# A deep fused kernel (RWKV-7, differential attention, two hybrid layers): tails and output stages in another order, table load behind the Silu, score matmuls by halves

## The reference

```python
def diff_attention_blocks(q, k_all, v_all, lam):      # 8 heads, each with two halves of 64
    s = jnp.einsum("bqhcd,bkhcd->bchqk", q_blk, k_all) * scale   # c: the two halves; 768 keys
    p = jax.nn.softmax(s, axis=-1)
    attn = p[:, 0] - lam * p[:, 1]
    return jnp.einsum("bhqk,bkhe->bqhe", attn, v_all)
def diff_finish(o, g, subln, lam_init, w_out):
    y = rms_norm(o, subln, SUBLN_EPS) * (1.0 - lam_init)
    return (y.reshape(B, T, DA_VW) * jax.nn.silu(g)) @ w_out
```

## Time and profile before

| | |
|---|---|
| runs (us) | 2391.37, 2387.86, 2383.27; median 2387.86 |
| the profiled execution, its time | 2388.85 us |
| its span, first to last instruction | 2387.0 us |
| mean granted TensorE clock | 0.962 of full speed |
| busy: PE, DVE, ACT, POOL | 86%, 55%, 47%, 30% |
| DMA | mean 93 GB/s |

### The profile page before, as it was taken

The page is one execution under the profiler, slowest core; times in us unless marked ns, Lnnn a source line. Parts: engine busy times, 40 slices in busy tenths (PEclk is TensorE's granted clock), DMA queues, the critical chain, the costliest instruction groups (busy, mean ns, idle before and its releaser), DMA issues.

```text
span 2387.0 us, 56898 instructions
## 1 busy us (share of the span) xinstructions
PE 2058.7 (86%) x24624; PEld 1583.7 (66%) x24624; DVE 1304.5 (55%) x2181; ACT 1118.4 (47%) x1861; POOL 708.8 (30%) x417
## 2 busy tenths in 40 slices
PE   6999998688878888878899999979899889899889
PEld 3877776567666677656676666647566666666666
DVE  3288787634334444443456667672566652466752
ACT  5476676433333343332354454553455453455552
POOL 2344544100022030233332222333433332443433
PEclk9999999899999999998999999989999989899999
DMA  7233646633332322223131111103222211222122
GB/s 298 89 121 122 185 131 186 184 99 91 113 102 72 83 67 74 60 96 124 60 105 55 54 45 58 54 23 115 75 67 79 65 61 71 71 80 71 62 71 71
DMA packets 162313, 221.35 MB, mean 93 GB/s; under 512 B 84592, under 2 KB 116336, under 8 KB 161296
## 3 DMA queue, kind: packets, MB, share of 16 engines
q1 hardware_dynamic: 151920, 177.99, 24.4%
q0 software_dynamic: 8992, 36.57, 5.1%
q10 hardware_dynamic: 1152, 3.15, 0.4%
HBM read 164.98 MB, written 42.21 MB: 87 GB/s over the span
## 4 chain that ended last, share of the span: by engine, by line
PE 57%; DVE 19%; ACT 12%; issue 8%; POOL 3%; DMA 1%; ACTq 0%; DVEq 0%; POOLq 0%; SPq 0%
PE ps L272 8%; PE ps L274 7%; PE ps L273 7%; PE ps L1605 3%; PE ps L1595 2%; PE ps L1627 2%; PE ps L421 2%; DVE Y L1768 2%; PE ps L2607 2%; PE ps L2545 1%; PE ps L3186 1%; ACT DE L1725 1%; ACT p L2627 1%; PE ps L3144 1%; DVE pc L3262 1%
## 5 line engine op out<-in xcount | busy, mean ns | idle before, releaser
L257 POOL TENSOR_TENSOR wbl<-wb,wbh 128x1024 fp32r<-128x1024 f32 x122 | 294.6, 2416 | 652.7 <-ACT wbh L251 652.7
L1768 DVE COPY_PREDICATED Y<-rc,ps 128x512 f32<-128x512 int32 x120 | 85.5, 732 | 196.3 <-ACT DE L1725 135.0
L272 PE MATMUL ps<-hT2h,wbh 128*128 128x512 f32 x416 | 180.5, 434 | 10.6 <-POOL wbl L257 10.6
L272 PE MATMUL ps<-hTh,wah 128*128 128x512 f32 (+1 forms) x512 | 179.5, 351 | 10.9 <-POOL wal L257 10.9
L273 PE MATMUL ps<-hTl,wah 128*128 128x512 f32 (+1 forms) x512 | 173.8, 340 | 0.0
L274 PE MATMUL ps<-hTh,wal 128*128 128x512 f32 (+1 forms) x512 | 173.6, 339 | 0.0
L274 PE MATMUL ps<-hT2h,wbl 128*128 128x512 f32 x416 | 164.6, 396 | 0.0
L273 PE MATMUL ps<-hT2l,wbh 128*128 128x512 f32 x416 | 164.0, 394 | 0.0
L1942 POOL TENSOR_TENSOR ro<-ro 128x768 f32<-128x768 f32 x6 | 10.9, 1813 | 496.8 <-DVE ro L365 496.8
L251 ACT ACTIVATE wbh<-wb 128x1024 fp32r<-128x1024 f32 x122 | 128.2, 1052 | 61.9 <-PE ps L2225 43.4
L257 POOL TENSOR_TENSOR wal<-wa,wah 128x1024 fp32r<-128x1024 f32 x34 | 104.0, 3059 | 175.8 <-ACT wah L251 175.8
(11 more groups left out here) (466 smaller groups left out, 5399.5 us busy)
## 6 DMA issues: line engine op xcount, KB each, us to landing
wb<-in_w_in SPq DMA_DIRECT2D x56, 512.0 KB, 3.5
wm<-in_ada SPq DMA_DIRECT2D x48, 512.0 KB, 5.7
s_str_dram<-s POOLq DMA_DIRECT2D x42, 576.0 KB, 8.7
bkv<-s_str_dram SPq DMA_DIRECT2D x96, 192.0 KB, 3.3
wa<-in_rw_in SPq DMA_DIRECT2D x34, 512.0 KB, 3.8
wb<-in_da_in SPq DMA_DIRECT2D x32, 512.0 KB, 3.5
ARI<-s_str_dram SPq DMA_DIRECT2D x96, 128.0 KB, 3.6
wb<-in_w_out SPq DMA_DIRECT2D x16, 512.0 KB, 3.5
```

The costliest lines, as they stand in the source:

```text
L257: e.tensor_tensor(lo, self.raw[:, n % 3], hi.bitcast(F32), ALU.subtract).then_inc(self.K.s.w_lo, 1)
L272: e.matmul(z, wh[:, k, :], hi[:, k, a:b], start=k == 0, stop=False)
L1768: e.copy_predicated(self.Y[:, l - 1], twice(self.mY[l - 1]), banks[:, :, 0:256]).then_inc(v, 1)
```

## The change

In eight places:

1. `products_ahead`: blocks j = 0 and 1 first with k = 0 to 5, then (0, 6), (1, 6), then block 2.
2. `act_project` of both classes: `K.exp_ln` directly behind the Silu.
3. `Diff.pe_attend`: in heads 0 to 6 the score matmuls alternate between the halves, and both halves' waits come before the first matmul.
4. Head 7: the end of head 6 (`pe_end`, `act_end`, `dve_sums`, `dve_end`, `pool_end`) comes later and uses bank 2; ScalarE copies the first transposes before it does the exps of blocks 2 and 3; `ahead` one or two steps later; ScalarE squares the last head from PSUM ahead of copying it.
5. Last pair of a layer: four parts before the second scores; the split of blocks 81 to 83 (121 to 123) at steps 1, 3, 5 of ScalarE in place of 0, 1, 2.
6. Output stages: x's square first; the memory's sums at k = 2, 4, 5; its tail five (GpSimd three) steps at k = 6 and at k = 7; the splits of blocks 84 to 89 at the end of iterations 1 to 6 (ScalarE) and the start of them (GpSimd), where they were at the start of iterations 3 to 7 and behind the loop.
7. The memory's second load waits for the seventh pair's values, and stands behind load 82 in the queue; it waited for the eighth y, behind load 83.
8. The memory's second buffer lies elsewhere.

```diff
 def products_ahead(K, e, W, n, x, banks, free, ready):
-    for j, bank in enumerate(banks):
-        e.wait_ge(K.s.w_lo, W.lo0 + n + j + 1)
-        free(j)
-        for k in range(7):
-            ready(k)
-            product_part(K, e, W, n + j, x, k, bank)
-            yield
+    for j, k in [(j, k) for j in range(2) for k in range(6)] + [(0, 6), (1, 6)] + [(2, k) for k in range(7)]:
+        if k == 0:
+            e.wait_ge(K.s.w_lo, W.lo0 + n + j + 1)
+            free(j)
+        ready(k)
+        product_part(K, e, W, n + j, x, k, banks[j])
+        yield
...
         e.activation(self.gb[b][:, :], psum[:, (i + 8) % 3, :], ACT.Silu).then_inc(s.evac_a, 1)
+        K.exp_ln(e)
         yield
...
+            if h < 7:
                 for a0, a1 in ((0, 512), (512, 768)):
-                    m = e.matmul(out[:, a0:a1], q[64 * cc:64 * cc + 64, 128 * qt:128 * qt + 128],
-                                 k[64 * cc:64 * cc + 64, a0:a1], start=True, stop=True)
-                m.then_inc(s.sc_mm, 1)
+                    for cc in range(2):
+                        m = score(qt, cc, a0, a1)
+                        if a0:
+                            m.then_inc(s.sc_mm, 1)
...
         for qt in range(4):
-            if qt < 2:
+            if qt < 2 and h < 7:
                 scores(qt + 2)
             yield
...
             e.activation(self.aT[b][:, 0:4, 128 * qt:128 * qt + 128],
                          psum[:, 3, :].rearrange("p (n c) -> p n c", c=128), ACT.Copy).then_inc(s.tr_a, 1)
+            if qt < 2 and h == 7:
+                scores(qt + 2)
+                if qt == 0:
+                    self.act_end(e, 6)
             yield
...
+        if h == 7:
+            e.wait_ge(s.pv_n, h)
+            e.activation(self.sq[2][:, :], psum[:, 2, :], ACT.Square).then_inc(s.pv_sq, 1)
+            e.activation(self.x2[:, h, :], psum[:, 2, :], ACT.Copy).then_inc(s.pv_c, 1)
+            yield
+            return
...
         e.activation(self.gb[b][:, :], psum[:, (i + 5) % 3, :], ACT.Silu).then_inc(s.evac_a, 1)
+        K.exp_ln(e)
         yield
...
-            if P % 8 == 7 and z:
-                run(some(ahead, 2))
+            if P % 8 == 7:
+                run(some(ahead, 2 if z else 4))
...
-        if P % 8 == 7:
-            self.W.split_hi(e, self.block(P) + 5)
         for z, _ in enumerate(self.steps(lambda z: (exponent(z), exponent(z + 1)), lambda z: None, finish)):
-            if P % 8 == 7 and z in (1, 2):
-                if z == 2:
+            if P % 8 == 7 and z in (1, 3, 5):
+                if z == 5:
                     e.wait_ge(s.nr_mul, o["nr_mul"] + self.scaled(P + 1))
-                self.W.split_hi(e, self.block(P) + 5 + z)
+                self.W.split_hi(e, self.block(P) + 5 + z // 2)
...
         for k in range(8):
-            if k >= 3:
-                self.W.split_hi(e, 81 + 40 * l + k)
             if l < 1:
+                e.wait_ge(s.evac_v, ev + k + 1)
+                nx.act_square(e, k)
                 if k == 0:
                     e.wait_ge(s.mem_in, 16 * l + 32)
-                if k < 3:
-                    for m in range(3 * k, min(3 * k + 3, 8)):
-                        nm.act_square(e, m)
-                else:
-                    run(some(tail, 2))
-                e.wait_ge(s.evac_v, ev + k + 1)
-                nx.act_square(e, k)
+                for m in {0: (0, 1, 2), 3: (3, 4, 5), 4: (6, 7)}.get(k, ()):
+                    nm.act_square(e, m)
+                if k >= 6:
+                    run(some(tail, 5))
+            if 0 < k < 7:
+                self.W.split_hi(e, 83 + 40 * l + k)
         if l < 1:
-            self.W.split_hi(e, 89 + 40 * l)
             run(nx.act_tail(e))
...
-            if k >= 3:
-                run(some(tail, 2))
+            if k >= 6:
+                run(some(tail, 5))
...
         for k in range(8):
-            if k >= 3:
-                self.W.split_lo(e, 81 + 40 * l + k)
-            if k >= 3:
-                run(some(tail, 1))
+            if 0 < k < 7:
+                self.W.split_lo(e, 83 + 40 * l + k)
+            if k >= 6:
+                run(some(tail, 3))
         if l < 1:
-            self.W.split_lo(e, 89 + 40 * l)
             run(self.nx[l + 1].pool_tail(e))
...
-            if n == 83:
-
-                e.wait_ge(s.yt_lo, self.c0["yt_lo"] + 8)
+            if n == 82:
+
+                e.wait_ge(s.pv_mm, self.c0["pv_mm"] + 7)
                 e.dma_start(self.mem[1][:, :, :], K.T["mem"]).then_inc(s.mem_in, 16)
```

More of the change, by code:

```diff
@@ L2531, in fill, with score @@
                 run(some(ahead, n))
+        def score(qt, cc, a0, a1):
+            return e.matmul(self.scored(h, qt, cc)[:, a0:a1], q[64 * cc:64 * cc + 64, 128 * qt:128 * qt + 128],
+                            k[64 * cc:64 * cc + 64, a0:a1], start=True, stop=True)
         def scores(qt):
@@ L2553, in values @@
             e.wait_ge(s.tok_c, 2 * h + 2)
+            e.wait_ge(s.rb_m, self.rb.done(h - 1))
             out = psum[:, 2, 128 * qt:128 * qt + 128]
@@ L2563, in turn @@
                 e.wait_ge(s.sm_df, 4 * z + 4)
-                if qt == 0 and h:
+                if qt == 0 and 0 < h < 7:
                     e.wait_ge(s.rb_m, self.rb.done(h - 1))
@@ L2587, in pe_attend @@
                 fill(2)
+            if qt == 0 and h == 7:
+                self.pe_end(e, 6)
             yield
@@ L2613, in pe_end, with sums @@
         e.wait_ge(s.pv_sq, h + 1)
-        self.rb.pe(e, h, K.psum[:, 3, :], K.ones, self.sq[2][:, :])
+        self.rb.pe(e, h, self.sums(h), K.ones, self.sq[2][:, :])
+    def sums(self, h):
+        return self.K.psum[:, 2 if h == 6 else 3, :]
     def act_attend(self, e, h):
@@ L2646, in act_attend @@
         e.wait_ge(s.pv_mm, h + 1)
-        e.activation(self.x2[:, h, :], psum[:, 2 if h == 7 else 3, :], ACT.Copy).then_inc(s.pv_c, 1)
+        if h == 7:
+            e.wait_ge(s.pv_n, h)
[3 more added lines that the diff above has]
+            return
+        e.activation(self.x2[:, h, :], psum[:, 3, :], ACT.Copy).then_inc(s.pv_c, 1)
         e.wait_ge(s.pv_c, h + 1)
@@ L2654, in act_end @@
     def act_end(self, e, h):
-        self.rb.act(e, h, self.K.psum[:, 3, :], self.R[2][:, :], 1e-5, 128.0)
+        self.rb.act(e, h, self.sums(h), self.R[2][:, :], 1e-5, 128.0)
     def dve_attend(self, e, h):
@@ L2700, in dve_attend @@
                 turn(qt - 1)
-            if qt == 0 and h:
+            if qt == 0 and 0 < h < 7:
                 self.dve_end(e, h - 1)
+            if qt == 1 and h == 7:
+                self.dve_sums(e, 6)
             if qt < 2:
                 scores(qt + 2)
+            if qt == 1 and h == 7:
+                self.dve_end(e, 6)
             yield
@@ L2716, in dve_end @@
         e.wait_ge(s.rb_r, self.rb.done(h))
+        e.wait_ge(s.pv_c, h + 1)
         e.scalar_tensor_tensor(out=self.x2[:, h, :], in0=self.x2[:, h, :], scalar=K.sm[:, 68:69],
@@ L2720, in pool_attend @@
     def pool_attend(self, e, h):
-        for _ in range(4):
-            yield
-        if h:
-            self.pool_end(e, h - 1)
-        for _ in range(7):
+        for z in range(11):
+            if h and z == (6 if h == 7 else 4):
+                self.pool_end(e, h - 1)
             yield
@@ L2761, in together @@
         for _ in attend(7):
-            if 0 < h < 4:
-                ahead(40 + h)
+            if 2 < h < 6:
+                ahead(38 + h)
             if 0 < h < 8:
@@ L2836, in __init__ @@
         with ExitStack() as cl:
-            self.mem = [K.sb(cl, "mem0", [8, 256], at=diff.end), K.sb(cl, "mem1", [8, 256])]
+            self.mem = [K.sb(cl, "mem0", [8, 256], at=diff.end)]
             for l in range(2):
@@ L2843, in __init__ @@
                                     self.nx[0] if l else None))
+                if l == 0:
+                    self.mem.append(K.sb(cl, "mem1", [8, 256]))
                 self.nm.append(Norm(K, cl, "nm", "m", self.mem[l], 256, [(0, 256, 0)], Am, None, self.hm, 3, False,
@@ L3321, in pe_out @@
                                lambda j: e.wait_ge(s.evac_v, ev + k - 2)))
-            if l < 1 and k < 3:
-                for m in range(3 * k, min(3 * k + 3, 8)):
-                    self.nm[l + 1].pe_sum(e, m)
             if l < 1 and k:
                 self.nx[l + 1].pe_sum(e, k - 1)
+            if l < 1:
+                for m in {2: (0, 1, 2), 4: (3, 4, 5), 5: (6, 7)}.get(k, ()):
+                    self.nm[l + 1].pe_sum(e, m)
         if l < 1:
```

13 lines of the change are left out of this document (7 added, 6 removed).

## The result

| | before | after |
|---|---|---|
| median of the runs (us) | 2389.45 (2383.27 to 2391.37) | 2430.49 (2427.38 to 2433.83) |
| the profiled execution: its time, its span | 2388.85, 2387.0 | 2430.78, 2429.0 |
| mean granted TensorE clock | 0.962 | 0.956 |

The ratio is 1.0177, with a 95% interval of 1.0153 to 1.0200: 42 us slower, where the forecast was 27 and its range ended at 2429.

A forecast was written before the change was run, and what follows sets the result against it. TensorE, busy 86% of the span, was taken as the bound, so its idles counted. 15.0 + 4 + 5 - 4.6 - 4.5 - 0.5 + 12.4 = +26.8 on 2388.85 gave 2415.7; forecast 2415 us, range 2395 to 2429.

The forecast's parts named there:

- Part 1: Heads 0 to 6: alternating score matmuls between halves changes nothing, 0 us, with bounds of 6.6 us gain or loss.
- Part 2: Table load behind the Silu: idle at twelve pair boundaries, 1.25 us each, +15.0; half clock at one in five, +4.
- Part 3: Last pair of each layer: idle of 3.9 us replaces 4.28, last-y wait opens, 2.5 us lost per layer, +5.
- Part 4: Head 7: third block's transposes 4.2 us earlier, 0.6 from the Square, less a 0.2 wait for y, -4.6 us.
- Part 5: Front of output stages: before layer 2 the memory's load wait goes, -4.5 us; before layer 1 only order, -0.5.
- Part 6: End of both inner output stages: GpSimd's split before the memory's low halves delays the last sum, 6.2 us each, +12.4.
- A: Rival: the load was in the boundary chain, so moving it gains 17.9 us instead of costing 19; 2379 us, chance 0.09.
- B: Rival: pair-boundary delays are swallowed by idles later in a pair, neither gain nor loss; 2396 us, chance 0.11.
- D: Rival: in heads 0 to 6 matmuls keep program order, so alternating halves gains 31 us; 2384 us, chance 0.03.
- C: Rival: at the output stages' end the low halves come in time, while pair boundaries still cost; 2403 us, chance 0.10.
- E: Rival: the moves do nothing on balance, TensorE's work is unchanged and waits only change place; 2388 us, chance 0.05.
- F: Rival: TensorE at half clock at most pair boundaries and after every new idle; 2428 us, chance 0.07.

The follow-up runs named there:

- experiment 2: b_load2 plus three extra matmuls ahead of each pair's values: ratio 1.0057; its estimate of the delay's price without half clock is 14 us in all.
- a_tail2: Kernel after with the memory's sums at k = 1, 2, 3 and its tail from iteration 3, splits kept in their new place: ratio 1.0117.
- experiments 1 and 7: Pairs' table load alone, out of the kernel after (1.0056) or into the kernel before (1.0093); score alternation in heads 0 to 6 alone in before (1.0005).
- experiment 1: Pairs' table load alone: back in front of the exp in the kernel after, 1.0056; moved behind the Silu in the kernel before, 1.0093.
- b_load2: Kernel before with only the pairs' table load moved directly behind the Silu: ratio 1.0093.

## Why the prediction was right and wrong

The direction was right, and so were most of the mechanisms: of the things listed to look for, each was found, but head 7 was only 2.5 us shorter. The sum was 15 us short, nearly all of it in one term, half clock at the boundaries.

- **Part 1, 0:** right. Heads 0 to 6 +0.6, alone +0.7.
- **Part 2, idle at the boundaries, 15.0:** right. The idle was right to the hundredth (2.16 us), and so nearly was the net price, 14 us by the estimate of experiment 2. That was partly luck: periods two to five cost 0.9 to 1.2 us, not 1.25, since up to 0.48 comes back (1.42 less 0.94), more than the 0.17 of the earlier trace rows; and the sixth costs 1.8, where a late weight split comes into view. The seventh is swallowed as forecast, by the idle of 4.28 us that becomes 2.86.
- **Part 2, half clock, 4:** this step failed. "If one boundary in five or so falls to 1.2 GHz" was a guess with the bounds 0 and 14, and I took a value near the low one. What the runs show: some 11 us with the load alone (24.8 less 14), and 18 in the pairs of the kernel after (34.8 less 16.6; 15 by the other traces of the same pairs), where the third and fourth periods of each layer fall to half clock too. The row that should have set it was there: a layer's last pair, with a single idle of 4.28 us, ran at 0.90. With 14 for 15.0 and 18 for 4 the sum comes to 2428 us, against 2430.5.
- **Part 3, +5:** 6.7 between the traces, 9.5 in the undoing, 4.5 timed; both new idles as forecast. By the undoing it was short, in part because the forecast priced the parts one by one: beside the load's delay the idle that the early parts were to fill is 2.76 us, not 4.28.
- **Part 4, -4.6:** -2.5 (-2.5 to -3.3 over eight traces). I had the transposes of the third block at 27.7 us after head 7's first scores (1606.1 less 1578.4); they start at 27.75 (1598.65 less 1570.90). That step was right to 0.1 us; the forecast left out what stands behind an idle of 8.04 us. The twelve values matmuls took 2.76 us where the kernel before needed 1.50, and from these transposes to the last block's values it is 12.95 us in place of 10.97: half clock took back 2.0 of the 4.2 in this trace.
- **Part 5, -4.5 and -0.5:** the memory's load gives 6.0 in its stage, timed 0.9975. Before layer 1 an order of the sums like the new one, with the early tail, gave nothing: 49.6 us in a_tail2, 49.3 before the change.
- **Part 6, +12.4:** right in mechanism and nearly in size. The stage before layer 1 is +7.3; undoing the late tail gives 7.0 there and 6.6 in the other. The forecast laid the whole on the split in front of the low halves; the split is worth 3.6, and the late tail without it would still cost as much.

Rivals: A, B and D are out by experiments 1 and 7, C by the idle of 6.48 us, E by experiment 1. F, "half clock at most boundaries and after every new idle", named what was missing and the nearest time, 2428, and had a chance of 0.07; "most" is too much, since at periods 1 to 5 of b_load2 none showed. The stage up to head 0 holds the same instructions and took 1216.1 to 1232.1 us over all seventeen traces, 1216.1 in the kernel after. Over the ten traces of kernels made from the one after its median is 1220.7, over the seven made from the one before 1224.2. So of the -8.0 in the table -3.5 may be real and the rest is scatter; with the 3 us that the pairs stand high, the +50 behind head 0 and the timed +42 then meet within 2 us or so. What moves that stage was not tried.

## What to carry to other kernels

Before an operation is moved on an engine, look at what stands behind its new place and who waits for that: 1.28 us of table load cost 22 to 29 us in front of a copy that TensorE waited for, and moving it behind that copy, from its old place, gained about 5. Price a new idle on TensorE with its clock, not as one row's length: here, in the pairs, half clock cost as much again as the delay itself. And when a norm's tail is pushed to the end of a stage, count what the next stage's start needs from the same three engines.

## What the runs showed of the hardware

- An idle of 2.16 us between long busy stretches was followed by a stretch at 1.2 GHz, worth 1.7 us, or was not, with the same instructions around it (clock 0.57 or 1.00 in the 4 us behind it). An extra 0.9 us of matmuls at the start of the layer changed which ones were, and made periods of 38.2 and 38.0 us into 39.9 and 39.7.
- Matmuls whose result is thrown away, put into such idles, made a kernel 8.6 us faster (1.0093 to 1.0057), as the granted clock rose from 0.84 to 0.95 in periods 6 and 7 of layer 1 and from 0.89 to 1.00 in its last pair; in periods 1 to 5, already at 1.00, they changed nothing.
- Half clock can hide a wait: where TensorE ran the work ahead of it at 1.2 GHz, the wait for a weight split showed as no idle, and at 2.4 GHz the same wait showed as 2.6 us.
- Of two score matmuls on different halves of the rows (64 each), the second started within 0.05 us of the first, ahead of three others that stand before it in the program.
- A load of the activation table took 1.28 us and the next operation began 0.01 us behind it.
